# RWKV's group norm and latent attention's normalisation at other places of a hybrid block

## The chip, the cores and the metric

The kernel runs on one NeuronCore of one Trainium2 chip. The metric is the device time of one execution in microseconds (us), the median of several runs; less is better. TensorE is called PE below, VectorE DVE, ScalarE ACT, GpSimd POOL, as in the profile.

## The reference

The reference is a stack of four layers on 256 tokens of width 1024, all in float32. Layers 0 and 1 are attention layers with an MLP; they are not touched. Layers 2 and 3 (the "second block") are hybrids: three branches share one input projection, are normalised each in its way, multiplied by a gate, and go through one output projection. Cut to what matters:

```
for layer in range(DEPTH):
    h = rms_norm_2(x, norm_g[layer])
    cols = split_columns(h @ w_in[layer])
...
    mix = jnp.concatenate([y_gdn.astype(F32), y_mla.astype(F32), y_rwkv.astype(F32)], axis=-1)
    mix = mix * jax.nn.silu(cols['gate'].astype(F32))
    x = x + mix.astype(x.dtype) @ w_out[layer]
return rms_norm_2(x, final_norm_g)

# gdn_branch, its end: an RMS norm over each of 6 heads of 64
o = rms_norm_2(bidir_merge(o), norm_g)

# mla_branch: 6 heads of 64
    s = jnp.einsum('bqhd,bkhd->bhqk', q_blk, k)
    p = jax.nn.softmax(s, axis=-1)
    return jnp.einsum('bhqk,bkhd->bqhd', p, v)

# rwkv7_branch, its end: a group norm over each of 4 heads of 64, then the bonus
y = bidir_merge(jnp.moveaxis(y, 0, 1))
mean = jnp.mean(y, axis=-1, keepdims=True)
var = jnp.mean(jnp.square(y - mean), axis=-1, keepdims=True)
y = ((y - mean) * lax.rsqrt(var + RWKV_LN_EPS)).reshape(b, l, RWKV_W) * ln_g.astype(F32) + ln_b.astype(F32)
...
return y + bonus.reshape(b, l, RWKV_W)
```

The mix has 1024 columns: 0 to 383 the delta rule (y_gdn), 384 to 767 latent attention (y_mla), 768 to 1023 RWKV. The delta rule needs, for 24 systems (2 directions, 2 chunks of 128 tokens, 6 heads), the inverse of a unit triangular 128x128 matrix. The kernel builds it from 16x16 blocks upwards, in three levels.

## The kernel before, in words

The program is written engine by engine: each engine's block is a straight list of instructions, in an order written out by hand, and semaphores order the engines against each other. `say` issues an instruction that signals a named event and waits until it is done, `step` and `tt` do the same on an engine's own counter, so DVE and ACT run one instruction after the other. An engine never passes over a wait: what stands behind it stays there.

Tokens lie in T = 2 tiles of 128 partitions. Matmul results go to 8 PSUM banks of 512 columns. `open_(key, ring)` (line 389) takes the next bank of a ring and makes PE wait until the last holder of that bank has been read by its reader. The rings are "unit" (banks 0 to 3), "five" (0 to 4), "fill" (4, 5), "long" (6, 7) and others; they are entered in turn. `transposes` opens one bank, `warm` writes an identity product to the next bank and does not take it.

For L in (2, 3) the stretch around the change is this:

- `invert(("g", L), "g", ...)`, the delta rule's inverse. On PE it is line 829 (16x16 base), then for levels 0 and 1 the products Y (line 840) and Z (line 853), then level 2 (lines 864, 873, 884). DVE masks and scales the blocks between them: `level_matrix` (2222), the late blocks (2277), the update from the banks of Z (2290), `early_blocks` (1824, the line of `tt`), the reads of VT (2306). A callback `between` puts other work into the gaps: `mla_between` on PE and ACT, `gdn_between` on DVE. Through it latent attention's scores (1156), transposed probabilities (1165) and products with v (1174, into the two banks `mO` of ring "long") run, and in DVE's callback the maxima (`mla_max`, 2600), `rwkv_variance` (from 2555) at ("Z", 0), and `rwkv_finish` with the delta gate's gain `gq` at ("Z", 2).
- The output stretch, `for n in range(2)`. It walks the two chunks: n = 0 opens its banks in "five", n = 1 in "unit". PE: KS (1226, only n = 1), U (1235), GS (1243, only n = 0), PU (1255). DVE answers: KS w = 0 times a decay and the right sides (2672, 2674), U (2678), KS w = 1 (2684 and an add), PU (2691 copies for n = 0, 2693 adds for n = 1, then the squares and their sums, 2696).
- `mla_finish` on DVE divides latent attention's sums (2657 reads the banks `mO`) and applies the gate. It stands in n = 1 between the right sides and the read of U.
- The output projection, `out_part(t, first, last, ks)` (line 1202, its matmuls are line 1209): for tile t and the k slices `ks` of 128 mix columns, two column halves, each into one of the accumulators, which it opens at `first`: ring "fill" for t = 0, ring "long" for t = 1. In `ks`, 0 to 2 are the delta rule, 3 to 5 latent attention, 6 and 7 RWKV. Each group needs its slice transposed first: mixR (RWKV, one bank for both tiles), mixM and mixG (one bank for each tile), by PE (line 431), copied to `hnT` by ACT (line 1366, `copy_out`).
- `residual` (1850) adds the four accumulators to x; the next layer's norm, or the last norm and the store, follow.

An instruction of float32 with 512 columns appears in the profile as two matmul records, so `out_part` with two slices is 8 records of line 1209 and with three slices 12.

Of the kernel before, what the change touches and what calls it, by code (L numbers as in the profile page):

```python
# [266 lines left out]
def program(nc, a, out, known=None):  # L267
    ctx = ExitStack()
    with ctx:
# [116 lines left out]
        def _(pe):  # L386
# [551 lines left out]
            for L in (2, 3):  # L938
# [277 lines left out]
                for n in range(2):  # L1216
# [20 lines left out]
                    if n == 0:  # L1237
                        mla_values(4)
                        for d, c in chunks:
                            pe.wait_ge(*at("bank_read_by_vector", "U", L, d, n))  # L1240
                            b = open_(("GS", ("g", L, d)), ring)
                            for h in range(6):
                                ins = mm(view(ps, b + (h // 2) * 64, (1, 64), p0=64 * (h % 2), np_=64),  # L1243
                                         view(R, GKD + d * 384 + h * 64, (1, 64)), view(R, GU + d * 384 + h * 64, (1, 64)), start=True, stop=True)
                            close(ins, ("GS", ("g", L, d)))
                        mla_values(5)
                        pe.wait_ge(*at("intra_masked", L, 0))
                    else:
                        pe.wait_ge(*at("bank_read_by_scalar", "mixR", L))
                        out_part(0, True, False, (6, 7))  # L1250
                    for d, c in chunks:
# [5 lines left out]
                        close(ins, ("PU", L, d, n))  # L1257
                    if n == 0:
                        transposes(("mixR", L), [view(R, MIXB + t * D + k * P, (1, P)) for k in (6, 7) for t in range(T)], "v",
                                   [at("rwkv_mix_ready", L)], ring)  # L1260

                def mix_part(name, t, ks, ready):
                    transposes((name, L, t), [view(R, MIXB + t * D + k * P, (1, P)) for k in ks], "v", [at(ready, L, t)], "unit")
                for t in range(T):
                    mix_part("mixM", t, (3, 4, 5), "mla_mix_ready")
                out_part(1, True, False, (6, 7))
                for t in range(T):
                    pe.wait_ge(*at("bank_read_by_scalar", "mixM", L, t))
                    out_part(t, False, False, (3, 4, 5))
                    mix_part("mixG", t, (0, 1, 2), "mix_ready")  # L1270
                for t in range(T):
                    pe.wait_ge(*at("bank_read_by_scalar", "mixG", L, t))
                    out_part(t, False, True, (0, 1, 2))

# [75 lines left out]
        def _(act):  # L1350
# [247 lines left out]
            for L in (2, 3):  # L1598
# [156 lines left out]
                def mla_between(what, n):  # L1755
# [11 lines left out]
                    elif n == 2:  # L1767
                        copy_out(view(hn, MPT(4 + (what == "Z")), (1, 512)), "mPT", L, 4 + (what == "Z"))
                        if what == "VT":
                            gate_tanh(0, 1)  # L1770
                            nc.scalar.preload_act_table_set("natural_log_exp_and_others")
                            act.wait_ge(*at("rwkv_var_ready", L))
                            rstd(RSS, 8, 1.0 / 64, 1)
                            act.sem_inc(up("rwkv_rstd_ready", L)[0], 1)
                invert(("g", L), "g", mla_between)
                act.wait_ge(*at("state_cleared", L))
                for d in (1, 0):
# [4 lines left out]
                    say(A(view(hnT, o + 64, (P, 3), (1, 64), p0=64, np_=64), view(ps, b, (64, 3), (1, 64), p0=64, np_=64), ACT.Copy),  # L1782
                        read("scalar", "GS", tag))
                copy_out(view(hnT, 6 * S, (1, 512)), "mixR", L)

                def mix_part(name, t, k):
                    copy_out(view(hnT, k * S + t * P, (S, 3), (1, P)), name, L, t, dims=((P, 3), (1, P)))
                for t in range(T):
                    mix_part("mixM", t, 3)
                for t in range(T):  # L1790
# [3 lines left out]
                for t in range(T):  # L1794
                    mix_part("mixG", t, 0)
                if L == 2:
                    layer_weights(1)
# [4 lines left out]
        def _(dve):  # L1802
# [513 lines left out]
            for L in (2, 3):  # L2316
# [291 lines left out]

                def rwkv_finish():

                    dve.wait_ge(*at("rwkv_rstd_ready", L))
                    tt(y8, y8, view(sm, RSS, (1, 8), (0, 64)), MUL)
                    yv = view(R, RY, (256, 2), (1, 256))
                    tt(yv, yv, view(rows, R_LNG + 256 * (L - 2), (0, 2), (1, 256)), MUL)
                    tt(yv, yv, bonus, ADD)
                    tt(view(R, MIXB + 768, (D, 2), (1, 256)), yv, view(R, GATE + 768, (D, 2), (1, 256)), MUL)
                    signal("rwkv_mix_ready", L)
                    gq = view(R, GATE, (D, 2), (64, 6), (1, 64))
                    tt(gq, gq, view(rows, R_GN + 64 * (L - 2), (0, 2), (0, 6), (1, 64)), MUL)

                def gdn_between(what, n):
# [10 lines left out]
                    if (what, n) == ("Z", 0):  # L2632
                        mla_max(3)
                        rwkv_variance()
                    if (what, n) == ("early", 1):
# [7 lines left out]
                    if (what, n) == ("Z", 2):  # L2643
                        gate_mul(0, 1)
                        rwkv_finish()
                invert(("g", L), "g", True, gdn_between)
# [16 lines left out]
                for n in range(2):  # L2663
# [4 lines left out]
                    if n == 1:  # L2668
                        for d, c in chunks:
# [4 lines left out]
                            say(V.tensor_tensor(r_, view(R, GN + c * 768 + 384, (1, 384)), r_, SUB), up("delta_rhs_ready", L, d))  # L2674
                        mla_finish()
                    for d, c in chunks:
                        b = full(dve, "U", L, d, n)
                        say(V.tensor_tensor(view(R, GU + d * 384, (64, 6), (1, 64)), view(ps, b, (64, 6), (1, 64)),
                                            view(sm, GBT + c * 12 + d * 6, (1, 6), (0, 64)), MUL), read("vector", "U", L, d, n))
                    if n == 1:  # L2680
                        for d, c in chunks:
                            b = full(dve, "KS", L, d, 1)
                            o = view(R, MIXB + c * D, (1, 384))
                            say(V.tensor_tensor(view(R, GT2, (64, 6), (1, 64)), view(ps, b, (64, 6), (1, 64)), gam(d, c), MUL),
                                read("vector", "KS", L, d, 1))
                            tt(o, o, view(R, GT2, (1, 384)), ADD)
                    for d, c in chunks:
                        o = view(R, MIXB + c * D, (1, 384))
                        b = full(dve, "PU", L, d, n)
                        if n == 0:  # L2690
                            say(V.tensor_copy(o, view(ps, b, (1, 384))), read("vector", "PU", L, d, n))
                        else:
# [3 lines left out]
                            step(V.tensor_reduce(view(sm, SS + 6 * c, (1, 6)), view(R, GR + c * 384, (64, 6), (1, 64)), AX.X, ADD))  # L2696
                            signal("gdn_ss_ready", L, c)
                for t in range(T):
                    dve.wait_ge(*at("gdn_rstd_ready", L, t))
                    o = view(R, MIXB + t * D, (64, 6), (1, 64))  # L2700
                    tt(o, o, view(sm, SS + 6 * t, (1, 6), (0, 64)), MUL)
                    o = view(R, MIXB + t * D, (1, 384))
                    tt(o, o, view(R, GATE + t * D, (1, 384)), MUL)
                    signal("mix_ready", L, t)
                residual(L, 1, TILES, "mix" if L == 2 else "fin", L + 1)
            for t in range(T):
# [31 lines left out]
```

## Time and profile before

| | |
|---|---|
| median of 3 runs | 1298.08 us (1293.09 to 1298.2) |
| the profiled execution | 1295.21 us, span of its instructions 1293.3 us |
| busy, share of the span | PE 95%, PE weight loads 68%, DVE 58%, ACT 27%, POOL 4% |
| granted TensorE clock, mean of the span | 0.992 |
| HBM read, written | 146.95 MB, 1.07 MB |

A row of the timeline is start, duration, engine, line, operation, operands, count, and in brackets the idle time of the engine before it and what released it. Rows of several instructions are merged. PE's durations overlap, since matmuls are pipelined: the distance from start to start is what one costs. The stretch of layer 3 stands in the rows; layer 2 shows the same 272.4 us earlier.

### The profile page before, as it was taken

The page shows a single profiled execution, that of the slowest core. Times are in us where ns is not written, and L with a number is a line of the kernel's source. Part 1 is how long each engine was busy: PE and PEld are TensorE (multiplying, and loading weights), DVE is VectorE, ACT ScalarE, POOL GpSimd, SP SyncE. Part 2 cuts the span into 40 slices and gives each one's busy share as a digit, 9 for nine tenths or more (in the row PEclk, how much of TensorE's full clock was granted, in tenths as well). Part 3 has the DMA queues.
Part 4 walks back from the last instruction along what each step waited for, and adds up shares of the span by engine and source line. Part 5 has one row for each costly group of instructions (what it writes and reads, how often), then busy time and mean ns, then how long its engine had stood idle before and what let it go on. Part 6 is the DMA issues. An engine that isn't in the chain of part 4 may idle for free. (4 is left out here: it accounts for less than half of the span.)

```text
span 1293.3 us, 18494 instructions
## 1 busy us (share of the span) xinstructions
PE 1229.6 (95%) x7285; PEld 878.4 (68%) x7285; DVE 749.8 (58%) x1467; ACT 345.8 (27%) x748; POOL 51.9 (4%) x92
## 2 busy tenths in 40 slices
PE   6999999999999999999999999999899999998997
PEld 5877549995447674699844478657566686575683
DVE  3254466775352145676743549875884378848872
ACT  2253312120012144121100222333441232434422
POOL 1100000000000000000000000200300000203000
PEclk9999999999999999999999999999999999999999
DMA  9731105454553431354544433310010632300000
GB/s 297 255 121 66 65 15 209 168 181 150 190 186 125 145 130 66 131 194 137 192 176 151 177 116 129 130 67 2 1 51 1 205 139 80 131 2 1 2 2 33
DMA packets 65853, 149.25 MB, mean 115 GB/s; under 512 B 2097, under 2 KB 8135, under 8 KB 65767
## 3 DMA queue, kind: packets, MB, share of 16 engines
q1 hardware_dynamic: 62432, 141.63, 31.0%
q0 software_dynamic: 1216, 3.52, 1.0%
q10 hardware_dynamic: 2119, 2.91, 0.9%
q8 instruction: 59, 0.97, 0.3%
q14 instruction: 27, 0.22, 0.1%
HBM read 146.95 MB, written 1.07 MB: 114 GB/s over the span
## 5 line engine op out<-in xcount | busy, mean ns | idle before, releaser
L1366 ACT ACTIVATE region<-banks 128x384 f32<-128x384 f32 (+8 forms) x159 | 77.0, 484 | 304.1 <-PE banks L442 105.0
L442 PE MATMUL banks<-hnT,weight_slabs 128*128 128x256 f32 x576 | 126.6, 380 | 3.4 <-DVE hnT L1841 3.4
L442 PEld LDWEIGHTS banks<-hnT,weight_slabs 128*128 128x128 f32 x576 | 108.8, 190 | 20.1 <-DVE hnT L1841 4.1
L494 PE MATMUL banks<-weight_slabs,region 128*128 128x512 f32 x256 | 115.1, 592 | 0.0
L494 PEld LDWEIGHTS banks<-weight_slabs,region 128*128 128x128 f32 x256 | 48.5, 190 | 60.3 <-issue 60.3
L494 PE MATMUL banks<-region 128*128 128x512 f32 x192 | 87.6, 592 | 0.0
L1824 DVE TENSOR_TENSOR region<-weight_slabs 128x1024 f32<-128x1024 f32 x32 | 39.2, 1225 | 80.3 <-PE banks L494 76.4
L1824 DVE TENSOR_TENSOR region<-region 128x256 f32<-128x256 f32 (+23 forms) x160 | 75.7, 473 | 17.1 <-ACT region L1711 12.0
L1982 DVE TENSOR_TENSOR region<-banks,region 128x128 f32<-128x128 f32 x40 | 11.7, 292 | 117.8 <-PE banks L609 91.2
L1824 DVE TENSOR_TENSOR region<-weight_slabs,region 128x1024 f32<-128x1024 f32 x64 | 78.2, 1221 | 1.1
L1322 POOL TENSOR_TENSOR region<-region,consts 128x240 f32<-128x240 f32 (+24 forms) x60 | 34.4, 599 | 957.1 <-DVEq L1833 934.2
L494 PEld LDWEIGHTS banks<-region 128*128 128x128 f32 x192 | 36.5, 190 | 45.9 <-issue 45.9
L482 PE MATMUL banks<-hn,region 128*128 128x128 f32 x512 | 62.6, 275 | 1.6 <-DVEq L1833 1.6
L482 PE MATMUL banks<-hn,weight_slabs 128*128 128x128 f32 x512 | 62.4, 275 | 0.0
L482 PEld LDWEIGHTS banks<-hn,region 128*128 128x128 f32 x512 | 59.7, 192 | 2.0 <-DVEq L1833 2.0
L1403 ACT ACTIVATE region<-region 128x1024 f32<-128x1024 f32 x16 | 16.9, 1059 | 163.8 <-DVEq L1833 163.8
L482 PE MATMUL banks<-hnT,weight_slabs 128*128 128x128 f32 x512 | 60.1, 275 | 0.0
L482 PEld LDWEIGHTS banks<-hn,weight_slabs 128*128 128x128 f32 x512 | 59.7, 192 | 0.0
L561 PE MATMUL banks<-hnT,weight_slabs 128*128 128x256 f32 x256 | 59.6, 384 | 0.0
L482 PEld LDWEIGHTS banks<-hnT,weight_slabs 128*128 128x128 f32 x512 | 58.8, 192 | 1.0 <-issue 1.0
L1209 PE MATMUL banks<-weight_slabs,hnT 128*128 128x512 f32 x128 | 56.4, 593 | 0.0
L1430 ACT ACTIVATE region<-region,small 128x128 f32<-128x128 f32 x80 | 36.5, 456 | 66.6 <-DVEq L1833 65.1
(363 smaller groups left out, 2050.7 us busy)
## 6 DMA issues: line engine op xcount, KB each, us to landing
weight_slabs<-in_mlp_w SPq DMA_DIRECT2D x32, 2048.0 KB, 8.7
weight_slabs<-in_w_in SPq DMA_DIRECT2D x10, 2048.0 KB, 7.8
weight_slabs<-in_od_w_in SPq DMA_DIRECT2D x6, 2048.0 KB, 8.1
weight_slabs<-in_ev_w_in SPq DMA_DIRECT2D x4, 2048.0 KB, 11.1
weight_slabs<-in_w_out SPq DMA_DIRECT2D x4, 2048.0 KB, 8.4
weight_slabs<-in_ev_w_out SPq DMA_DIRECT2D x2, 2048.0 KB, 8.0
weight_slabs<-in_od_w_out SPq DMA_DIRECT2D x2, 2048.0 KB, 7.7
weight_slabs<-in_w_in SPq DMA_DIRECT2D x2, 2016.0 KB, 7.5
```

Source lines behind the costliest of these rows:

```text
L442: ins = mm(view(ps, b + i * S, (1, S)), view(slabs, o + k * width + c0, (1, P)), view(hnT, k * S, (1, S)), start=k == 0, stop=k == KC - 1)
L482: ins = mm(view(ps, b + j * P, (1, P)), view(w, wt + k * step_ + j * P, (1, P)), view(act[0], act[1] + k * act[2], (1, P)), start=k == 0, ...
L494: ins = mm(view(ps, b, (1, 512)), view(R, act + k * st, (1, P)), view(w, wt + k * step_, (1, 512)), start=n == 0 and k == 0, stop=n == 7 a ...
L561: ins = mm(view(ps, b + i * S, (1, S)), view(slabs, o + k * width + c0, (1, P)), view(hnT, k * S, (1, S)), start=k == 0, stop=k == KC - 1)
L1209: ins = mm(view(ps, acc[t, n], (1, 512)), view(hnT, k * S + t * P, (1, P)), view(slabs, o + k * 512, (1, 512)), start=first and k == ks[0] ...
L1322: nc.gpsimd.tensor_tensor(view(R, W.row(k), (w * W.NS, 2), (w, W.NS), (1, w)), view(R, W.A + k + 1, (16 * W.NS, 2), (16, W.NS), (1, w)), v ...
L1366: say(A(dst, view(ps, b, *(dims or ((1, n),)), np_=np_), ACT.Copy, scale=scale), read("scalar", *key))
L1403: step(A(view(R, ZR, (1, 1024)), view(R, ZR, (1, 1024)), ACT.Relu))
L1430: ins = A(v, v, ACT.Exp, scale=0.125, bias=view(sm, MX(i) + t, (1, 1)), accum_out=view(sm, SU(name, h) + t, (1, 1)))
L1824: step(V.tensor_tensor(o, p_, q, op))
L1982: go(V.tensor_tensor(v[0], view(ps, b, (1, P)), view(R, BT + bh * S + P - 1, (-1, P)), ADD))
```

## The change

Nothing of the arithmetic changes. On DVE, `rwkv_variance` goes from ("Z", 0) of the delta rule's inverse to the end of n = 0's reads of U; `rwkv_finish` is cut in two, `rwkv_scale` (times the reciprocal deviation, times the gain) behind n = 0's reads of PU, and the rest (bonus, gate) where `mla_finish` stood in n = 1. `gq` stays at ("Z", 2). `mla_finish` goes behind the delta rule's last normalisation, just ahead of `residual`. The delta rule's sums lie in region GP and no longer in MIXB. ACT's `rstd` for RWKV moves from the inverse to behind the copies of GS, and its mixG copies come before its mixM copies. On PE the transposes mixR go from the end of n = 0 (ring "five") to just before `out_part(0, True, False, (6, 7))` in n = 1 (ring "unit"); after the loop `out_part(1, True, False, (6, 7))` comes first, then for each tile mixG, its `out_part`, and the transposes mixM, and last the two `out_part` of latent attention.

```diff
@@ PE
                     else:
+                        transposes(("mixR", L), [view(R, MIXB + t * D + k * P, (1, P)) for k in (6, 7) for t in range(T)], "v",
+                                   [at("rwkv_mix_ready", L)], ring)
                         pe.wait_ge(*at("bank_read_by_scalar", "mixR", L))
                         out_part(0, True, False, (6, 7))
...
-                    if n == 0:
-                        transposes(("mixR", L), [view(R, MIXB + t * D + k * P, (1, P)) for k in (6, 7) for t in range(T)], "v",
-                                   [at("rwkv_mix_ready", L)], ring)
...
-                for t in range(T):
+                out_part(1, True, False, (6, 7))
+                for t in range(T):
+                    mix_part("mixG", t, (0, 1, 2), "mix_ready")
+                    pe.wait_ge(*at("bank_read_by_scalar", "mixG", L, t))
+                    out_part(t, False, False, (0, 1, 2))
                     mix_part("mixM", t, (3, 4, 5), "mla_mix_ready")
-                out_part(1, True, False, (6, 7))
                 for t in range(T):
                     pe.wait_ge(*at("bank_read_by_scalar", "mixM", L, t))
-                    out_part(t, False, False, (3, 4, 5))
-                    mix_part("mixG", t, (0, 1, 2), "mix_ready")
-                for t in range(T):
-                    pe.wait_ge(*at("bank_read_by_scalar", "mixG", L, t))
-                    out_part(t, False, True, (0, 1, 2))
+                    out_part(t, False, True, (3, 4, 5))
@@ ACT
-                            act.wait_ge(*at("rwkv_var_ready", L))
-                            rstd(RSS, 8, 1.0 / 64, 1)
-                            act.sem_inc(up("rwkv_rstd_ready", L)[0], 1)
...
+                act.wait_ge(*at("rwkv_var_ready", L))
+                rstd(RSS, 8, 1.0 / 64, 1)
+                act.sem_inc(up("rwkv_rstd_ready", L)[0], 1)
                 copy_out(view(hnT, 6 * S, (1, 512)), "mixR", L)
...
-                for t in range(T):
-                    mix_part("mixM", t, 3)
...
                 for t in range(T):
                     mix_part("mixG", t, 0)
+                for t in range(T):
+                    mix_part("mixM", t, 3)
@@ DVE
-                def rwkv_finish():
+                yv = view(R, RY, (256, 2), (1, 256))
+
+                def rwkv_scale():
 
                     dve.wait_ge(*at("rwkv_rstd_ready", L))
                     tt(y8, y8, view(sm, RSS, (1, 8), (0, 64)), MUL)
-                    yv = view(R, RY, (256, 2), (1, 256))
                     tt(yv, yv, view(rows, R_LNG + 256 * (L - 2), (0, 2), (1, 256)), MUL)
+
+                def rwkv_finish():
+
                     tt(yv, yv, bonus, ADD)
                     tt(view(R, MIXB + 768, (D, 2), (1, 256)), yv, view(R, GATE + 768, (D, 2), (1, 256)), MUL)
                     signal("rwkv_mix_ready", L)
-                    gq = view(R, GATE, (D, 2), (64, 6), (1, 64))
-                    tt(gq, gq, view(rows, R_GN + 64 * (L - 2), (0, 2), (0, 6), (1, 64)), MUL)
...
                         mla_max(3)
-                        rwkv_variance()
...
                         gate_mul(0, 1)
-                        rwkv_finish()
+                        gq = view(R, GATE, (D, 2), (64, 6), (1, 64))
+                        tt(gq, gq, view(rows, R_GN + 64 * (L - 2), (0, 2), (0, 6), (1, 64)), MUL)
...
-                        mla_finish()
+                        rwkv_finish()
...
+                    if n == 0:
+                        rwkv_variance()
                     if n == 1:
...
+                    if n == 0:
+                        rwkv_scale()
...
                     signal("mix_ready", L, t)
+                mla_finish()
                 residual(L, 1, TILES, "mix" if L == 2 else "fin", L + 1)
```

## Rows read from the trace of the kernel before

**Rows 1.** The page: busy us, share of the span and instructions of each engine.
```profile
PE 1229.6 (95%) x7285; PEld 878.4 (68%) x7285; DVE 749.8 (58%) x1467; ACT 345.8 (27%) x748; POOL 51.9 (4%) x92
```

**Rows 2.** The chain that ended last, in order of time: start, duration, what.
```profile
1274.77 10.32 PE banks L1209 x24
```

**Rows 3.** Timeline of PE, the levels of layer 3.
```profile
1213.73 0.88 PE L853 MATMUL banks<-region 64*64 64x16 f32 x24
...
1216.00 1.12 PE L422 MATMUL banks<-consts 128*128 128x512 f32 x2
1218.01 0.89 PE L840 MATMUL banks<-region 64*64 64x32 f32 x24 [0.89 <-issue]
```

**Rows 4.** Timeline of DVE, the levels of layer 3.
```profile
1212.02 0.69 DVE L2555 TENSOR_REDUCE small<-region 128x8 f32<-128x512 f32 x1
...
1214.40 0.69 DVE L2559 TENSOR_REDUCE small<-region 128x8 f32<-128x512 f32 x1
1215.24 1.28 DVE L2290 SCALAR_TENSOR_TENSOR region<-banks,consts,region 128x96 f32<-128x96 f32 x4
...
1217.29 0.56 DVE L1824 TENSOR_TENSOR region<-region,small 128x384 f32<-128x384 f32 x1
...
1222.84 0.69 DVE L2600 TENSOR_REDUCE small<-banks 128x2 f32<-128x512 f32 x1 [1.43 <-PE banks L1156]
```

**Rows 5.** Timeline of DVE, the end of the inverse and n = 0.
```profile
1238.78 1.42 DVE L1824 TENSOR_TENSOR region<-region 128x512 f32<-128x512 f32 x2
...
1241.34 1.15 DVE L2678 TENSOR_TENSOR region<-banks,small 128x384 f32<-128x384 f32 x2
...
1247.35 0.56 DVE L2691 COPY region<-banks 128x384 f32<-128x384 f32 x1 [0.78 <-PE banks L1255]
```

**Rows 6.** Timeline of PE, the output stretch of layer 3.
```profile
1247.08 0.61 PE L431 MATMUL banks<-consts,region 128*128 128x128 f32 x4
1248.05 2.92 PE L1226 MATMUL banks<-hnT,region 128*128 128x128 f32 x24 [0.37 <-DVE region L2691]
...
1253.43 3.65 PE L1209 MATMUL banks<-weight_slabs,hnT 128*128 128x512 f32 x8
1256.92 2.79 PE L1255 MATMUL banks<-region 128*128 128x64 f32 x24
...
1268.80 0.49 PE L431 MATMUL banks<-consts,region 128*128 128x128 f32 x3
```

**Rows 7.** Timeline of DVE, n = 1 of layer 3.
```profile
1249.07 0.56 DVE L2672 TENSOR_TENSOR region<-banks,small 128x384 f32<-128x384 f32 x1 [1.16 <-PE banks L1226]
...
1251.43 0.17 DVE L1827 TENSOR_SCALAR small<-small 128x12 f32<-128x12 f32 x1
...
1251.90 1.15 DVE L2657 TENSOR_TENSOR region<-banks,small 128x384 f32<-128x384 f32 x2
...
1258.48 0.56 DVE L2693 TENSOR_TENSOR region<-banks,region 128x384 f32<-128x384 f32 x1 [0.47 <-PE banks L1255]
...
1264.14 0.56 DVE L1824 TENSOR_TENSOR region<-region 128x384 f32<-128x384 f32 x1
```

**Rows 8.** Timeline of ACT, its copies of mixR and of the first mixG.
```profile
1247.78 0.60 ACT L1366 ACTIVATE hnT<-banks 128x512 f32<-128x512 f32 x1 [3.08 <-PE banks L431]
...
1269.32 0.49 ACT L1366 ACTIVATE hnT<-banks 128x384 f32<-128x384 f32 x1 [6.59 <-PE banks L431]
```

**Rows 9.** Timeline of PE: its longest waits inside the span, with what follows.
```profile
745.71 1.09 PE L431 MATMUL banks<-consts,hn 128*128 128x128 f32 x8 [1.65 <-ACT hn L1567]
...
916.53 1.35 PE L1133 MATMUL banks<-mla_weights,region 128*128 128x384 f32 x2 [2.85 <-DVE region L2247]
```

**Rows 10.** Windows: length, busy PE, PEld, DVE, ACT, POOL, clock, DMA share, GB/s.
```profile
740.00:750.00 10.00, 6.82 (x32) 4.57 (x33) 4.81 (x6) 5.57 (x13) 0.00 (x0) 1.00 0.06 23
...
912.00:922.00 10.00, 6.55 (x20) 4.01 (x18) 8.99 (x21) 4.45 (x11) 3.66 (x8) 0.83 0.00 0
...
1289.00:1293.00 4.00, 0.00 (x0) 0.00 (x0) 1.10 (x1) 0.00 (x0) 0.00 (x0) 0.50 0.44 179
```

More of the change, by code:

```diff
@@ L1257, in _ @@
                         close(ins, ("PU", L, d, n))
-                    if n == 0:
-                        transposes(("mixR", L), [view(R, MIXB + t * D + k * P, (1, P)) for k in (6, 7) for t in range(T)], "v",
-                                   [at("rwkv_mix_ready", L)], ring)
                 def mix_part(name, t, ks, ready):
                     transposes((name, L, t), [view(R, MIXB + t * D + k * P, (1, P)) for k in ks], "v", [at(ready, L, t)], "unit")
-                for t in range(T):
-                    mix_part("mixM", t, (3, 4, 5), "mla_mix_ready")
                 out_part(1, True, False, (6, 7))
                 for t in range(T):
-                    pe.wait_ge(*at("bank_read_by_scalar", "mixM", L, t))
-                    out_part(t, False, False, (3, 4, 5))
-                    mix_part("mixG", t, (0, 1, 2), "mix_ready")
-                for t in range(T):
-                    pe.wait_ge(*at("bank_read_by_scalar", "mixG", L, t))
-                    out_part(t, False, True, (0, 1, 2))
+                    mix_part("mixG", t, (0, 1, 2), "mix_ready")
+                    pe.wait_ge(*at("bank_read_by_scalar", "mixG", L, t))
+                    out_part(t, False, False, (0, 1, 2))
+                    mix_part("mixM", t, (3, 4, 5), "mla_mix_ready")
+                for t in range(T):
+                    pe.wait_ge(*at("bank_read_by_scalar", "mixM", L, t))
+                    out_part(t, False, True, (3, 4, 5))
         def full(eng, *key):
@@ L2682, in _ @@
                             b = full(dve, "KS", L, d, 1)
-                            o = view(R, MIXB + c * D, (1, 384))
+                            o = view(R, GP + c * 384, (1, 384))
                             say(V.tensor_tensor(view(R, GT2, (64, 6), (1, 64)), view(ps, b, (64, 6), (1, 64)), gam(d, c), MUL),
@@ L2687, in _ @@
                     for d, c in chunks:
-                        o = view(R, MIXB + c * D, (1, 384))
+                        o = view(R, GP + c * 384, (1, 384))
                         b = full(dve, "PU", L, d, n)
@@ L2697, in _ @@
                             signal("gdn_ss_ready", L, c)
+                    if n == 0:
+                        rwkv_scale()
                 for t in range(T):
                     dve.wait_ge(*at("gdn_rstd_ready", L, t))
-                    o = view(R, MIXB + t * D, (64, 6), (1, 64))
+                    o = view(R, GP + t * 384, (64, 6), (1, 64))
                     tt(o, o, view(sm, SS + 6 * t, (1, 6), (0, 64)), MUL)
-                    o = view(R, MIXB + t * D, (1, 384))
-                    tt(o, o, view(R, GATE + t * D, (1, 384)), MUL)
+                    tt(view(R, MIXB + t * D, (1, 384)), view(R, GP + t * 384, (1, 384)), view(R, GATE + t * D, (1, 384)), MUL)
                     signal("mix_ready", L, t)
+                mla_finish()
                 residual(L, 1, TILES, "mix" if L == 2 else "fin", L + 1)
```

## The prediction

> **What bounds the kernel now.** I read the page first, for who is busy; then the chain of waits, for who is last; then the timelines of PE, DVE and ACT over the two stretches that the diff touches. PE is busy for 95% of the span and DVE for 58% [rows 1]. The chain ends in line 1209, the output projection, at 24 records in 10.32 us, that is 0.43 us a record without a hole [rows 2]. So PE is the engine whose holes count; a DVE instruction costs something only where PE stands for it. Two such holes lie in the changed stretches. In the levels PE is idle for 0.89 us before the second Y product [rows 3]; the page puts it down to "issue", but DVE's last `early_blocks` instruction ends at 1217.85 and PE goes on at 1218.01, so it is DVE that it waits for [rows 3, 4]. In the output stretch it stands for 0.37 us before KS, for the DVE copy of the second PU bank (its row starts at 1247.35) [rows 5, 6]. Everything else in n = 1 and in the projection is back to back: what DVE does there is hidden. All times below are on the clock of the trace of before, in layer 3; each layer has the stretch once, so sums count twice.
>
> **Levels: what leaves.** `rwkv_variance` runs from 1212.02 to 1215.09 (1214.40 + 0.69), 3.07 us [rows 4]. Behind it the two updates from Z start at 1215.24 and take 1.28 [rows 4]. Z's first bank is full by then, its second at 1214.61 (1213.73 + 0.88) [rows 3]. Without the variance the first update is done before that; the second (half of 1.28) runs 1214.75 to 1215.4. From the end of the updates (1216.52) to the end of `early_blocks` (1217.85) are 1.33, so these are ready at 1216.7 and PE could go at 1216.85. PE itself gets there at 1216.00 + 0.95, the warm product's two records, = 1216.95 [rows 3]. So PE starts the Y product 1.06 earlier; the 0.89 of the row plus the overlap of pipelined ends. Does the gain stay? DVE's next dependence is the scores' bank, for which it waits 1.43 us [rows 4]; that comes from PE, so it moves 1.06 earlier with PE, and the DVE-bound rest of the inverse (masks, VT) is behind it. **-1.06 us.** `rwkv_finish` leaves the end of the inverse, four operations of about 0.71 [rows 5] of which all but the gate's gain move. DVE then waits there for U instead: it read U at 1241.34 [rows 5], but PE does attention's product of head 4 first and GS then, which are busy without a hole. Worth 0; the cover is PE's own list, and without it the gain would be 1 us at most.
>
> **n = 0.** The variance now runs from the end of the U reads (1241.34 + 1.15 = 1242.5) to 1245.6. PU's second copy starts at 1247.35 after 0.78 of waiting, so the first, 0.56 long, ran from 1246.0 to 1246.6 [rows 5]. So it fits into DVE's waiting time. 0. `rwkv_scale` follows the second copy: 1247.94 + 2 x 0.72 = 1249.4; KS was read at 1249.07 [rows 7], so DVE is 0.3 late. The moved `rstd` on ACT lies in ACT's idle time (it waited 3.08 before mixR [rows 8]). Its ready signal is due about 1246.2.
>
> **mixR, the first stall.** Before, its transposes (0.61) stood in front of KS and under the wait for the PU copy [rows 6]; taking them away gives nothing in layer 2, where KS opens the same bank, held by PU. In layer 3 ring "unit" has been turned one bank further (13 opens a layer for 12), KS opens banks that are free and starts 0.97 earlier, but U waits for DVE's right sides at 1250.6 and 1251.8, so nothing comes of it either. Now DVE: four KS operations to 1249.4 + 4 x 0.59 = 1251.8, `rwkv_finish` 2 x 0.72 to 1253.2, U reads 2 x 0.59 to 1254.4 [rows 5, 7]. mixR needs `rwkv_mix_ready` (1253.2), but also a bank: it is the seventh open of n = 1 in a ring of four, after KS x 4 and U x 2, so it takes the third one's, KS (d = 1, w = 1). DVE frees that only with its first operation behind the U reads, at 1255.0. PE is done with U at 1253.43 [rows 6] and starts mixR at 1255.15. ACT's copy starts 0.70 after the transposes (1247.78 - 1247.08) and takes 0.60 [rows 6, 8]; with 0.2 to start again (KS came 0.14 after DVE's copy [rows 5, 6], and weights are loaded first) `out_part(0)` begins at 1256.65 instead of 1253.43. **+3.22 us.** Queued behind it on PE: PU and all of the projection.
>
> **mO, the second stall and the largest term.** `out_part(1, True, ...)` opens its accumulators in ring "long", banks 6 and 7, and those are held by latent attention's `mO` until line 2657 has read them. Before, `mla_finish` read them at 1251.90 [rows 7], long before they were wanted. Now it is DVE's last piece, and `out_part(1)` comes straight after PU. PE: PU begins at 1256.65 + 3.49 = 1260.14 and takes 24 x 0.11 = 2.6, so PE wants bank 6 at 1262.75. DVE: its first add from PU came 1.56 after PU's start (1258.48 - 1256.92), and from there to the end of the delta rule's mix are 6.22 (1264.14 + 0.56 - 1258.48) [rows 6, 7]. That gives 1261.70 and 1267.92; then 0.47 for the reciprocals (1251.90 - 1251.43) and 0.56 for the first read [rows 7]: bank 6 is free at 1268.95 and PE resumes at 1269.1. Bank 7 follows 0.6 later, earlier than its 1.7. **+6.35 us**, PE standing still, with everything that is left behind it. It is no deadlock: DVE's mix needs nothing of PE after PU.
>
> **mixG.** Each group of three transposes (0.32 from start to start) was followed by another tile's matmuls, which hid ACT's copy [rows 6]. Now PE waits for the copy at once: 0.52 until it starts (1269.32 - 1268.80), 0.49 for it, 0.2 to resume: 1.2 for 0.32 [rows 6, 8]. Twice: **+1.8 us**. The mixM transposes lie behind matmuls as before; `mla_mix_ready` (1269.0 + 1.8) precedes them by 5 us. The closing pair of `out_part` and the tail are the same.
>
> **The clock.** The granted clock is full in both changed stretches. PE stood for 2.85 us before 916.53 [rows 9], and in the ten microseconds 912 to 922 the mean is 0.83, which is 3.4 us at the lower level, 1.2 GHz [rows 10]. After the last matmul (1274.77 + 10.32 [rows 2]) PE stays idle, and from 1289, 3.9 us later, the clock is at 0.50 [rows 10]. A wait of 1.65 before 745.71 leaves the window 740 to 750 at 1.00 [rows 9, 10]. A stall of 6.35 is far beyond 2.85; I take one such fall a layer, with its low phase on matmuls: 3.4 us at half rate costs **+1.7 us**, between 0 (it is over in the stall) and 3.4 (two). The Trainium skill (TensorE: Matmul & The Clock Gate, "Why this matters for your kernels") has a rule that speaks against this change: between bursts of matmuls leave no long idle gap, or the array falls back to the half clock. By that rule the sum has the clock term in it, and without it the sum is that of (a) below; the trace agrees at 916.
>
> **The sum.** A layer: -1.06 + 3.22 + 6.35 + 1.8 = +10.3, and +1.7 for the clock: 12.0. Two layers: 24.0. On the profiled execution's own 1295.2 us (span 1293.3; the median of the runs shown is 1298.1, 0.2% more) that is 1319.2, 1.9% more.
>
> **Rivals.** (a) The same stalls without the clock's loss: 1295.2 + 20.6 = 1315.8; with twice its loss: 1322.6. (b) PE doesn't stand for bank 6, because the banks or the order are other than I read them: 3.22 + 1.8 - 1.06 = 4.0 a layer, 1303.1. For it: PE shows no wait on a "long" bank before. Against: the ring has two banks and both accumulators and `mO` use them. (c) The other side, not slower: the inverse is DVE's. DVE is busy in much of it and 5.9 us leave its list (3.07 and four times 0.71). If all of it shortened the layer and (b) held, a layer would be 5.9 - 5.0 = 0.9 shorter: 1293.4. It decides from a gain of 5.0 a layer in the levels. For it: DVE's dense rows there. Against: PE's hole before the Y product is only 0.89, and DVE waits 1.43 for PE right after [rows 3, 4]. (d) Only the mO stall and mixG are real, and mixR is hidden: 7.1 + 1.7 = 8.8 a layer, 1312.8. For it: 1.7 of its 3.22 is bank 1's order, which I counted.
>
> **How the numbers follow.** The forecast with its clock term 0.5, (a) 0.25, (d) 0.15, (b) 0.06, (c) 0.04. Predicted 1319.2. The range reaches from (d), less 3 for the spread of runs (before lie 5 apart), to two clock losses a layer on a run at the upper edge: 1310 to 1327. It leaves (b) and (c) out. What a measurement of this kernel can tell from no change is about 0.5%, 6.5 us. Slower 0.93; same 0.05, which is (c) and a mild (b); faster 0.02.
>
> **What would show it.** In the trace of after: PE idle for some 6 us before line 1209 behind the second PU of each layer, released by DVE's line 2657; about 1.7 us before the four transposes of mixR, and 0.9 before `out_part(0)`; 0.9 before the projection of each mixG; the hole before the Y product of level 1 gone; the clock under 1.0 in the windows after the long wait; DVE's variance between the U reads and PU. Wrong it would be if the long wait isn't there, if its length isn't near 6.35, or if the clock stays full.

## The result and the profile after

The changed kernel takes 1325.43 us (median of 4 runs, 1321.77 to 1329.97) where the kernel before took 1295.59 beside it: a ratio of 1.0225, 95% interval 1.0198 to 1.0253. In runs taken later, for the experiments (e8), it was 1.0203 (1.0179 to 1.0227), 1324.84 us against 1299.11. That is 29.8 us more in the first set and 25.7 in the second; the forecast was 24.0 more, 1319.2 in a range of 1310 to 1327. Ratios here and below are of fast runs; one run of all was slow, 1372.81 us at a mean clock of 0.901, with the kernel of e10.

The profiled execution took 1323.26 us, span 1321.4. The page's first lines show the shape of it: PE's busy time has grown by 8 us only [rows 1], the rest of the 28 is idleness, and the clock's row has three eights where it had none.

```profile
span 1321.4 us, 18490 instructions
...
PE 1237.9 (94%) x7285; PEld 880.4 (67%) x7285; DVE 749.4 (57%) x1467; ACT 346.8 (26%) x748; POOL 51.8 (4%) x92
...
PEclk9999999999999999999999999999988999999989
```

The timeline of PE in the output stretch of layer 2. It answers to [rows 6], 272.4 us earlier; line 1257 is the former 1255. The bracket is the idle time before the row.

```profile
970.95 2.84 PE L1257 MATMUL banks<-region 128*128 128x64 f32 x24
974.60 4.54 PE L1226 MATMUL banks<-hnT,region 128*128 128x128 f32 x24 [0.81 <-DVE region L2693]
978.98 2.79 PE L1235 MATMUL banks<-region 128*128 128x64 f32 x24
983.17 0.63 PE L431 MATMUL banks<-consts,region 128*128 128x128 f32 x4 [1.40 <-DVE region L2686]
984.49 5.40 PE L1209 MATMUL banks<-weight_slabs,hnT 128*128 128x512 f32 x8 [0.69 <-ACT hnT L1364]
989.72 2.79 PE L1257 MATMUL banks<-region 128*128 128x64 f32 x24
998.73 5.35 PE L1209 MATMUL banks<-weight_slabs,hnT 128*128 128x512 f32 x8 [6.21 <-DVE region L2657]
1003.91 0.49 PE L431 MATMUL banks<-consts,region 128*128 128x128 f32 x3
1004.98 5.42 PE L1209 MATMUL banks<-weight_slabs,hnT 128*128 128x512 f32 x12 [0.58 <-ACT hnT L1364]
1010.24 0.82 PE L431 MATMUL banks<-consts,region 128*128 128x128 f32 x6
1011.70 5.42 PE L1209 MATMUL banks<-weight_slabs,hnT 128*128 128x512 f32 x12 [0.65 <-ACT hnT L1364]
```

Four things are to be seen. The wait of 6.21 before `out_part(1)` is released by line 2657, the read of latent attention's banks. The 1.40 before mixR is released by line 2686, the read of KS w = 1, and not by the RWKV mix. Three copies of ACT (0.69, 0.58, 0.65) are waited for. And three rows are longer than the same work in [rows 6]: KS 4.54 for 2.92, the 8 records of `out_part` 5.40 and 5.35 for 3.65.

The reason for these three is in the granted clock. Windows of the changed kernel (columns as in [rows 10]), the first over the levels of layer 2, the others over its output stretch and that of layer 3:

```profile
932.00:974.00 42.00, 40.35 (x515) 30.45 (x514) 30.91 (x47) 19.43 (x50) 2.15 (x3) 1.00 0.12 39
974.00:979.00 5.00, 4.40 (x25) 4.43 (x26) 4.43 (x8) 0.00 (x0) 0.00 (x0) 0.66 0.00 0
984.00:990.00 6.00, 5.51 (x11) 2.49 (x12) 0.77 (x2) 0.44 (x1) 0.00 (x0) 0.72 0.01 3
994.00:1003.00 9.00, 4.27 (x6) 1.89 (x7) 5.73 (x12) 0.51 (x2) 0.00 (x0) 0.62 0.00 1
1267.00:1273.00 6.00, 4.79 (x11) 2.32 (x12) 2.04 (x4) 0.60 (x1) 0.00 (x0) 0.72 0.00 0
1278.00:1289.00 11.00, 6.21 (x8) 2.65 (x9) 5.79 (x12) 0.51 (x2) 0.00 (x0) 0.53 0.00 0
```

The granted clock has two levels here, 1.00 (2.4 GHz) and 0.50 (1.2 GHz). So a mean of 0.66 over 5 us is 3.4 us at 1.2 GHz ((1 - 0.66) x 2 x 5), 0.62 over 9 is 6.8, 0.53 over 11 is 10.3. Such a piece at 1.2 GHz is called a low phase below. The kernel before had a full clock in all of this stretch.

The same stretch by terms, in us against the kernel before, from start to start of rows, beside the forecast. "end of PU" is 2.63 us behind its start, the distance to the next row in the kernel before:

| term | layer 2 | layer 3 | forecast |
|---|---|---|---|
| first Y product to U of n = 0 (the levels) | -0.98 | -1.12 | -1.06 |
| PU of n = 0 to `out_part(0)` | +4.50, of it some 1.4 clock | +3.10 | +3.22 |
| `out_part(0)` itself, clock | +1.75 | +1.47 | in the clock's 1.7 |
| end of PU to `out_part(1)` | +6.38 | +6.37 | +6.35 |
| `out_part(1)` itself, clock | +1.74 | +3.07 | in the clock's 1.7 |
| the two mixG | +1.55 | +1.55 | +1.8 |
| first Y product to the last residual | +15.16 | +14.64 | +12.0 |

The terms leave 0.2 us a layer over, in rows that the table doesn't name. The two layers give 29.8; the rest of the program was 1.8 faster in that profile, where it had three phases of low clock before the tail and the kernel before five.

### The profile page after: what moved, and what is told of

Read it like the earlier page. It is cut to its first block and busy times, and to the rows that moved or that the text cites. A ratio compares the mean times of both kernels' runs of the same rounds, so it can differ in the third digit from the quotient of the medians.

```text
span 1321.4 us, 18490 instructions
## 1 busy us (share of the span) xinstructions
PE 1237.9 (94%) x7285; PEld 880.4 (67%) x7285; DVE 749.4 (57%) x1467; ACT 346.8 (26%) x748; POOL 51.8 (4%) x92
## 5 line engine op out<-in xcount | busy, mean ns | idle before, releaser
L494 PE MATMUL banks<-region 128*128 128x512 f32 x192 | 87.6, 592 | 0.0
L1209 PE MATMUL banks<-weight_slabs,hnT 128*128 128x512 f32 x128 | 65.1, 665 | 16.3 <-DVE region L2657 12.4
L1848 DVE TENSOR_TENSOR x_res<-banks,x_res 128x512 f32<-128x512 f32 x24 | 16.6, 692 | 76.9 <-PE banks L1209 51.6
```

The costliest lines, as they stand in the source:

```text
L494: ins = mm(view(ps, b, (1, 512)), view(R, act + k * st, (1, P)), view(w, wt + k * step_, (1, 512)), start=n == 0 and k == 0, stop=n == 7 a ...
L1209: ins = mm(view(ps, acc[t, n], (1, 512)), view(hnT, k * S + t * P, (1, P)), view(slabs, o + k * 512, (1, 512)), start=first and k == ks[0] ...
L1848: say(V.tensor_tensor(v, view(ps, b, (1, 512)), v, ADD), read("vector", *key))
```

## The experiments

e1 to e4 ran on one chip, beside a kernel before of 1299.1 us, e5 and e6 on a second, and e7 to e10 on a third. The changed kernel ran again only on the third (e8), so e1 to e4 are compared with it by their ratios to the kernel before and by the stretch.

In each the stretch from the start of the first Y product of the delta rule's inverse to the start of the last residual add was measured in its profile; it is 80.55 and 80.36 us in the kernel before (80.55 and 80.35 in a second profile of it), 95.7 and 95.0 in the changed one (95.2 and 95.8 in a second).

**The mO banks (e1).** `mla_finish` moves into DVE's wait for PU.

```diff
                             tt(o, o, view(R, GT2, (1, 384)), ADD)
+                        mla_finish()
...
                     signal("mix_ready", L, t)
-                mla_finish()
                 residual(L, 1, TILES, "mix" if L == 2 else "fin", L + 1)
```

> The changed kernel, with mla_finish moved on DVE from its last place into the gap in which DVE waits for the second PU banks (behind the adds of KS w = 1). Theory (PE stands for the mO banks): the wait of 6.21 us before out_part(1) of each layer goes, and the low clock behind it with it (1.7 in layer 2, 3.1 in layer 3): 12.4 + 4.8 less, about 1308 us; DVE's added 2.9 us lie in its 6.2 us of waiting for PU. Rival (the projection waits for the delta rule's mix just behind, the mO banks only happen to be named): the wait turns into one for mix_ready of nearly the same length, within 2 us of the changed kernel, about 1325.

Measured: 1310.2 us, ratio to the kernel before 1.0083 (1.0056 to 1.011), so 1.2 to 1.4% or 16 to 18 us are gone against the changed kernel's 1.0203 and 1.0225. The stretch is 87.6 and 87.5 us, 15.7 less in all where 17.2 was expected. PE after the second PU, layer 2:

```profile
993.94 2.79 PE L1257 MATMUL banks<-region 128*128 128x64 f32 x24
996.56 3.65 PE L1209 MATMUL banks<-weight_slabs,hnT 128*128 128x512 f32 x8
1000.46 0.55 PE L431 MATMUL banks<-consts,region 128*128 128x128 f32 x3 [0.24 <-DVEq L1831]
```

`out_part(1)` follows PU without a hole and at full clock, and only 0.24 us are left that PE waits for the delta rule's mix. The rival, which wanted the long wait to come back as that one, is out. It also shows that for this wait the order on PE was harmless; only the place of the banks' reader was not.

The clock is not full in all of the stretch. Windows over mixR and `out_part(0)`, and over what follows:

```profile
985.00:994.00 9.00, 6.81 (x14) 3.19 (x14) 5.59 (x12) 0.60 (x1) 0.00 (x0) 0.62 0.01 2
994.00:1010.00 16.00, 14.53 (x58) 8.05 (x57) 5.57 (x10) 2.48 (x7) 0.00 (x0) 1.00 0.00 1
1261.00:1270.00 9.00, 6.79 (x12) 3.28 (x13) 5.62 (x12) 0.60 (x1) 0.00 (x0) 0.62 0.00 0
```

With the long wait gone, a low phase of 6.8 us is left in each layer, around the hole of 1.62 and 1.73 us that mixR's bank makes. So a fall comes there without the long wait; e3 and e5, without that hole, have none there.

**The order on PE (e4).** DVE stays; PE opens the accumulators later.

```diff
-                out_part(1, True, False, (6, 7))
                 for t in range(T):
                     mix_part("mixG", t, (0, 1, 2), "mix_ready")
                     pe.wait_ge(*at("bank_read_by_scalar", "mixG", L, t))
+                    if t == 1:
+                        out_part(1, True, False, (6, 7))
                     out_part(t, False, False, (0, 1, 2))
```

> The changed kernel, with PE's order alone changed: out_part(1, True, ...) not right behind PU but behind the transposes of mixG for tile 1, so that mixG for tile 0 and its out_part come first. DVE's order is that of the changed kernel. Theory: PE now waits for mix_ready of tile 0, which comes 2.5 us before the mO banks are read: the hole is 3.7 in place of 6.2, 5 less in all plus a part of the clock's loss, about 1319. Rival (the whole wait is DVE's chain, whatever PE wants of it): within 1.5 us of the changed kernel.

Measured: 1324.05 us, 1.0203 (1.0151 to 1.0255). The interval doesn't tell 5 us from nothing; the trace does. The wait has become one for the mix, 3.80 long, as expected:

```profile
999.12 0.90 PE L431 MATMUL banks<-consts,region 128*128 128x128 f32 x3 [3.80 <-DVEq L1832]
```

The stretch is 93.6 and 91.7 us, 2.1 and 3.3 less than in the changed kernel, which is the 5 less of the theory. The clock gave next to nothing back: the profile has 13.7 us of low phase in layer 2, as much as the changed kernel has in each layer, and 10.2 in layer 3. The 12 records of `out_part(0)` behind the wait took 7.53 and 7.16 us for 5.42. So behind a hole of 3.8 the clock cost 2.1 and 1.7 us, behind the one of 6.2 it had cost 1.7 and 3.1.

**mixR's bank (e3).**

```diff
-                                   [at("rwkv_mix_ready", L)], ring)
+                                   [at("rwkv_mix_ready", L)], "five")
```

> The changed kernel, with mixR's bank taken from ring five and not unit, so that it no longer opens the bank of KS (d = 1, w = 1). Theory (it is that bank, and not rwkv_mix_ready, that mixR waits for): PE's holes of 1.40 and 1.73 us before mixR go, its start moves to about the end of U: 1.4 to 1.8 less a layer, 3.2 in all, and 0 to 1.7 more for a fall of the clock: about 1321. Rival (rwkv_mix_ready comes no earlier than the bank, or the mO wait eats the gain because it ends by DVE's clock): within 1 us of the changed kernel.

Measured: 1321.32 us, 1.0172 (1.0131 to 1.0212). Timeline of PE, layer 2:

```profile
981.95 2.92 PE L1226 MATMUL banks<-hnT,region 128*128 128x128 f32 x24 [0.81 <-DVE region L2693]
984.70 2.79 PE L1235 MATMUL banks<-region 128*128 128x64 f32 x24
987.33 0.61 PE L431 MATMUL banks<-consts,region 128*128 128x128 f32 x4
988.67 3.67 PE L1209 MATMUL banks<-weight_slabs,hnT 128*128 128x512 f32 x8 [0.73 <-ACT hnT L1364]
```

mixR runs right behind U: `rwkv_mix_ready` was there, the bank was not. From PU of n = 0 to `out_part(0)` it is 10.4 us in both layers where layer 3 of the changed kernel had 12.1, so 1.75 of the 3.1 are the bank. `out_part(0)` is at full clock too. The wait for mO is 6.21 as in the changed kernel: it moves along with PU, and doesn't eat the gain. The stretch is 90.6 and 91.6 us, 5.1 and 3.4 less than in the changed kernel; what goes beyond the wait is clock, since no low phase comes before the long wait.

**All three mended (e5).** `mla_finish` as in e1, mixR as in e3, and both mixG transposes ahead of the first `out_part` that needs one:

```diff
                 for t in range(T):
                     mix_part("mixG", t, (0, 1, 2), "mix_ready")
+                for t in range(T):
                     pe.wait_ge(*at("bank_read_by_scalar", "mixG", L, t))
```

> The changed kernel with three things undone: mla_finish in DVE's gap before the second PU, mixR in ring five, and both mixG transposes ahead of the first out_part that needs them. Theory: what is left against the kernel before is mixR's copy on ACT (1.5 a layer), the first mixG's copy and 0.3 of waiting (1.2), against the 1.06 that the levels give: 1.7 a layer, 3.4 in all, about 1299 us. Rival (the levels give nothing that lasts): 2.7 a layer, 1301; or the low clock stays and adds 1.7 a layer, 1302 to 1304.

Measured: 1304.66 us, 1.0038 (1.0017 to 1.0058) of a kernel before of 1299.54. No low phase in either stretch, which are 82.6 and 82.3: 2.1 and 1.9 over the kernel before, 1.7 expected. The third mending cost about what it gave, since mixG for tile 1 now waits 0.75 for DVE at a place where it used to be ready. The 4.0 of the two stretches lie in the interval of 2.2 to 7.5 us.

**The clock by itself (e2, e7).** Identity products keep PE busy in its holes; who waits for whom stays.

```diff
+                warm(6, "unit")
                 out_part(1, True, False, (6, 7))
```

> The changed kernel, with six products of the identity (0.95 us each) on PE just before out_part(1, True, ...), so that PE is busy while it waits for the mO banks; nothing else is different. Theory (the clock falls because PE stands there): the wait's end stays at the same distance from PU, the low clock after it is gone: 1.7 + 3.1 less, about 1320.5 us. Rival (the clock falls for the thin work of the whole stretch, the holes before it included): the low phase stays, 1325; or it moves only, within 1.5 us of the changed kernel.

e7 has that line and three more:

```diff
                     if n == 1:
+                        warm(1, "fill")
                         for w in range(2):
...
                     else:
+                        warm(1, "fill")
                         transposes(("mixR", L), [view(R, MIXB + t * D + k * P, (1, P)) for k in (6, 7) for t in range(T)], "v",
                                    [at("rwkv_mix_ready", L)], ring)
+                        warm(1, "fill")
                         pe.wait_ge(*at("bank_read_by_scalar", "mixR", L))
```

> The changed kernel, with identity products in each of its new holes on PE: one before KS of n = 1, one before and one behind mixR's transposes (ring fill, whose banks are free then), six before out_part(1, True, ...). All waits and their lengths stay. Theory (the low clock of the stretch comes from the four new holes together, not from the long one alone): no low phase between the levels and the end of the projection; the stretch from the first Y product to the last residual is 95.7 and 95.0 us in the changed kernel's profile and becomes 90.6 and 90.6, 9.5 less than the changed kernel run beside it. Rival (only the long hole lowers the clock): a phase stays around out_part(0), 1.7 to 3 us of the gain are missing in each layer.

> The changed kernel unchanged, to stand beside the others on one chip. By the sum of its own profile (10.2 a layer for the waits, 4.5 to 5.1 a layer for the clock) 29 us over the kernel before it on the same chip; rival: the clock's part differs from chip to chip, 22 to 27 or over 31.

e2 measured 1328.84 us, 1.0223 (1.0183 to 1.0263): by time, nothing gained. Its windows show both why, and that the theory holds for the place itself:

```profile
986.00:995.00 9.00, 6.70 (x15) 3.22 (x15) 3.34 (x6) 0.60 (x1) 0.00 (x0) 0.62 0.01 2
1000.00:1010.00 10.00, 8.41 (x22) 3.53 (x21) 5.48 (x12) 1.00 (x3) 0.00 (x0) 1.00 0.00 0
1285.00:1295.00 10.00, 8.41 (x22) 3.50 (x21) 4.70 (x10) 0.78 (x3) 0.00 (x0) 1.00 0.00 0
```

Around the filled wait the clock is full in both layers, and `out_part(1)` takes 3.70 us, near the 3.65 of the kernel before. The low phase around mixR is still there, 6.8 us long in layer 2 and 3.4 in layer 3. The stretch is 93.6 and 92.0, 5 less in all. In the profiled execution this is lost ahead of the stretch, which no edit touches: the first Y product of layer 2 starts at 938.33 us, where it starts at 932.08 and 933.30 in the two profiles of the changed kernel. For the other three runs there is no trace; their mean clock, 0.979 to 0.982, is no higher than the changed kernel's 0.978 to 0.982 in e8. So whether the fill gives its 5 us in every run stays open.

e7 measured 1318.59 us, 1.0154 (1.013 to 1.0178), and e8, the changed kernel beside it, 1324.84, 1.0203 (1.0179 to 1.0227). The stretches of e7, at full clock from end to end, are 91.0 and 90.6 us:

```profile
935.00:1026.00 91.00, 86.61 (x687) 55.46 (x686) 50.33 (x80) 25.77 (x64) 2.15 (x3) 1.00 0.11 33
1221.00:1312.00 91.00, 86.86 (x687) 55.52 (x686) 50.41 (x80) 25.76 (x64) 2.15 (x3) 1.00 0.01 1
```

So it is the new holes that lower the clock, and the stalls alone, less what the levels give, cost 10.4 and 10.3 us a layer (91.0 - 80.55, 90.6 - 80.36), for the forecast's 10.3. The mean clocks of all the runs say that this is not the chance of one profile: 0.986 to 0.990 in the five of e7, 0.978 to 0.982 in the five of e8. Against e8's profile the stretches are 9.4 us shorter, the medians 6.3. Beside one another on one chip, the changed kernel is 25.7 us over the kernel before, in the 22 to 27 that I had given to the rival of e8; the 29 of its theory still lies in the interval, 23.3 to 29.5. In e8's own profile the stretches are as long as in the first one (95.2 and 95.8), so what differs lies outside them, in the kernel before too: it took 1299.11 here and 1295.59 in the first set.

One row of e8 bears on how firm a fall is. KS of layer 2 stands behind the same hole of 0.81 as in the first profile, where it took 4.54:

```profile
975.83 2.92 PE L1226 MATMUL banks<-hnT,region 128*128 128x128 f32 x24 [0.81 <-DVE region L2693]
```

**Where the clock is low otherwise (e9).** The kernel before, profiled again on the chip of e7 and e8.

> The kernel before, profiled on the same chip, for where its clock is low: outside the changed stretch it should have the phases that the experiments show near 60 to 75, 145, 183, 880 and 1190 us, which no edit here touches; within the stretch none, 80.5 and 80.4 us long. Rival: these early phases belong to the edits, and are not there.

Measured: 1298.81 us, 1.0002 (0.9981 to 1.0023). Its profile:

```profile
60.00:66.00 6.00, 4.46 (x20) 3.35 (x20) 4.25 (x15) 1.50 (x7) 0.00 (x0) 0.72 1.05 386
144.00:155.00 11.00, 10.37 (x30) 6.92 (x31) 3.50 (x13) 5.46 (x16) 0.00 (x0) 0.53 0.01 2
935.00:1016.00 81.00, 78.42 (x669) 52.49 (x668) 50.39 (x81) 25.72 (x64) 2.15 (x3) 1.00 0.13 39
1211.00:1291.00 80.00, 77.65 (x667) 52.13 (x666) 50.14 (x80) 25.72 (x64) 2.14 (x3) 1.00 0.01 1
```

The low phases near 62, 144, 182, 875 and later belong to the program and come and go from run to run: in the profile shown first there was none at 62, and 3.4 us at 145 where there are 10.3 here. Within the changed stretch there is none. The wait of 2.85 us at 916, from which the prediction took its fall, has none behind it in this profile:

```profile
921.33 0.91 PE L1133 MATMUL banks<-mla_weights,region 128*128 128x384 f32 x2 [2.84 <-DVE region L2247]
```

The window around it:

```profile
910.00:930.00 20.00, 15.28 (x79) 10.86 (x79) 17.80 (x37) 10.13 (x22) 9.93 (x15) 1.00 0.00 1
```

**The levels' part alone (e6, e10).** Can the 1.06 be had without the rest? In the kernel before, DVE waited 3.5 us behind the U reads of n = 0 (its row of layer 2):

```profile
973.62 0.56 DVE L2691 COPY region<-banks 128x384 f32<-128x384 f32 x1 [3.52 <-PE banks L1255]
```

There `rwkv_finish` fits (4 x 0.72), and the variance where `rwkv_finish` was.

```diff
                         mla_max(3)
-                        rwkv_variance()
...
                         gate_mul(0, 1)
-                        rwkv_finish()
+                        rwkv_variance()
+                        gq = view(R, GATE, (D, 2), (64, 6), (1, 64))
+                        tt(gq, gq, view(rows, R_GN + 64 * (L - 2), (0, 2), (0, 6), (1, 64)), MUL)
...
                                             view(sm, GBT + c * 12 + d * 6, (1, 6), (0, 64)), MUL), read("vector", "U", L, d, n))
+                    if n == 0:
+                        rwkv_finish()
```

> The kernel before, with rwkv_variance moved from Z of level 0 to the place where rwkv_finish stood at the end of the inverse, rwkv_finish behind the U reads of n = 0 (where DVE waited 3.5 us for PU), and ACT's rstd behind the inverse. PE's order, banks and mixR stay as before. Theory (the 1.06 us of the levels are PE's, and DVE's 5.9 us fit into its waits): 2.1 less than before, about 1293.5, PE's hole before the second Y product gone. Rival (DVE's list is the bound of the inverse, so the variance put back in it takes it all back): within 0.5 us of before.

> The kernel with only the levels' part again, on another chip. Its stretch was 79.6 and 79.2 us for 80.55 and 80.4, which is 2.1 less, but its time was 6 to 11 less. Theory (the rest was one or two low phases of the clock fewer, outside the stretch, by chance of the runs): 2 to 4 less than before here. Rival (the earlier start moves the phases of the clock for good, the gain is real): again 6 to 11 less.

Measured: e6 1291.38 us, 0.9933 (0.9912 to 0.9953); e10 1296.3 us, 0.997 (0.995 to 0.999) of 1299.11. The stretch is 79.6 and 79.2 in both profiles, 0.96 and 1.12 less than before in the one, 0.97 and 1.13 in the other. PE at level 1 (answers to [rows 3]: no hole before line 840), and DVE behind the inverse in e6:

```profile
940.07 0.60 PE L1165 MATMUL banks<-consts,region 128*128 128x128 f32 x4
940.51 1.02 PE L422 MATMUL banks<-consts 128*128 128x512 f32 x2
941.46 0.89 PE L840 MATMUL banks<-region 64*64 64x32 f32 x24
```
```profile
966.52 0.69 DVE L1824 TENSOR_TENSOR region<-region,small 128x512 f32<-128x512 f32 x1
967.25 0.69 DVE L1824 TENSOR_TENSOR region<-region,row_params 128x512 f32<-128x512 f32 x1
967.97 1.42 DVE L1824 TENSOR_TENSOR region<-region 128x512 f32<-128x512 f32 x2
969.75 0.56 DVE L2692 COPY region<-banks 128x384 f32<-128x384 f32 x1 [0.36 <-PE banks L1255]
```

The four operations end 0.36 before PU's first bank is there, so DVE waits for it as before. The gain of 2.1 us is real and was repeated; the 8 us of e6 were not, and e10 with its 2.8 agrees with the stretch. What e6 had above it lies outside the stretch, where its profile has four low phases of 3.4 us ahead of the tail and e9's has 34 us of them in all. This is the fastest of the kernels: 0.3% under the kernel before in the repeat.

## Why the prediction was right, and where it was off

- **Levels, -1.06: right.** -0.98 and -1.12 in the changed kernel, -0.96 to -1.13 in e6 and e10, where the rest of the change is absent and the variance is back in the inverse at a later place. DVE's chain after the scores moved along, as worked out; the inverse is not bound by DVE (rival c).
- **n = 0, nothing: right.** The variance ran between the U reads and PU, `rwkv_scale` delayed DVE by 0.3 in layer 2 of e8 (it reads KS at 977.17, 1.34 behind KS's start, for 1.02 in the kernel before).
- **mixR, +3.22: right**, 3.10 in layer 3. The bank counted was the right one: e3 took 1.75 of it away by a bank alone. Rival (d) is out.
- **mO, +6.35: right**, 6.38 and 6.37. e1 removed it by the reader's place. Rival (b) is out. Rival (a), the same stalls at full clock, is the kernel of e7 and not this one.
- **mixG, +1.8: 1.55.** ACT's copy lets PE go on with less than the 0.2 that I put in.
- **The clock, +1.7 a layer: this is the term that was mis-sized.** It was 4.9 and 4.5, 9.4 in all for 3.4, and makes up the 6 us between the forecast's 24.0 and the measured 29.8. The step that failed is "one such fall a layer": I had tied a fall to the length of the single longest wait, from 2.85 at 916 and from 1.65 at 745, behind which the clock held. In the changed kernel it fell at KS behind a hole of 0.81 and at `out_part(0)` behind 1.40 and 0.69, and again, for 6.8 and 10.3 us, at the long wait. e1 removed the long wait and e2 filled it, and both kept the fall around mixR; e7 filled all and left none. Of the short holes, mixR's is the one that goes with the fall: in the ten layers with mixR's hole of 1.4 to 1.7 us (the changed kernel twice, e1, e2, e4) the clock fell ahead of PU, and in the four with holes of 0.81 and 0.73 alone (e3, e5) it did not.

  The rule of the Trainium skill (TensorE: Matmul & The Clock Gate, "Why this matters for your kernels"), that long gaps between bursts of matmuls bring the half clock back, agrees with the long wait, of 6.2 us, at which the clock fell in all six of its layers (the changed kernel twice, e3). The rule names long gaps only; here the clock fell behind shorter holes too.

  The kernel before had a row that I left out of the argument: behind a wait of only 1.46 us, at 1140.86, its own clock was at 0.83 over 1140 to 1150. It lay as near to the new holes as the row at 745. And neither row that the term was taken from was firm: behind the wait of 2.85 the clock fell in the first profile and stayed full in e9, and behind the one of 1.65 it held in the first profile and fell in e5 (0.83 over 747 to 757). The row that was left out, and its window:

```profile
1140.86 2.48 PE L1049 MATMUL banks<-region 128*128 128x64 f32 x16 [1.46 <-ACT region L1595]
```
```profile
1140.00:1150.00 10.00, 9.14 (x88) 8.98 (x88) 1.31 (x5) 2.37 (x6) 0.00 (x0) 0.83 0.01 2
```

- **The range** took in twice the clock's loss, 1322.6, and on top of it a run at the upper edge. The loss was 2.8 times the forecast's, so it is this allowance for runs, and not the working, that kept 1325.4 inside; that was in part luck. In the second set, with 25.7 us more, it was not needed.

Still open: whether e2's 5 us are there in its unprofiled runs, why the hole of 0.81 lowered the clock in one profile of the changed kernel only, and how the clock's phases outside the stretch are drawn from run to run.

## What to carry to other kernels

When a step that reads a bank moves later on its engine, look up who opens that bank next, in the ring's own order: here both stalls were banks, and the data that the instructions really needed was there. Before taking work off a busy engine's list, find the row in which the bound engine waits for it (here 0.9 us of 5.9), and put it into a wait that is already there; e6 kept that gain and paid nothing. Price a new hole with its clock, and the short ones too: in layer 2 of the changed kernel the low phases at the holes of 0.7 to 1.4 us cost 3.2 us and the one at the hole of 6.2 cost 1.7; in layer 3 it was 1.5 and 3.1.

## What the runs showed of the hardware

The granted clock fell to 1.2 GHz for 3.4 us or more behind a hole of PE as short as 0.8 us in one profile, and not behind the same hole in the next: KS of layer 2 took 4.54 us in the one profile of the changed kernel and was at full clock in the other. Even a wait of 2.84 us in layer 2, ahead of any edit, was followed by a fall in some profiles (the kernel before, e3) and by none in others (e9, e8). The same program before the change had 17.1 us of low clock ahead of its tail in one profile (five phases of 3.4, 1295.21 us) and 34.1 in another (e9, 1301.47 us), and its runs beside e7 to e10 lie between 1292.6 us at a mean clock of 0.992 and 1304.9 at 0.984. So a part of the spread of such a kernel's times is this, and a change of 2 us is seen in a stretch of the trace sooner than in a median.
